# A mixture-of-experts loop with a fifth weight slot, and second-layer weights requested by ScalarE

## What is computed

```python
scores = sigmoid(x @ router_w)                       # 64 experts
eidx = top_8(group_limited(scores + router_bias))    # 8 experts per token
wts = sel / sum(sel) * 2.5
hb = silu(einsum('nd,edf->nef', xb, ex_w1)) * einsum('nd,edf->nef', xb, ex_w3)
routed = einsum('nef,efd->nd', hb * gates[..., None], ex_w2)
shared = einsum('nf,fd->nd', silu(x @ sh_w1) * (x @ sh_w3), sh_w2)
```

## Time and profile before

| | before |
|---|---|
| median of 3 runs | 1056.3 us |
| the profiled execution | 1055.14 us, its span 1053.4 us |
| mean granted TensorE clock | 0.986 |
| PE busy | 997.3 us, 95% of the span |
| DVE / ACT / POOL busy | 448.9 / 156.4 / 356.7 us |
| expert loop, from first to last matmul | 365.5 to 957.8 us |
| weights of the experts, from SyncE | 192 requests of 1024 KB |
| gathers and scatters, GpSimd's queue | 200 and 48 instructions, 37.8 MB |
| SyncE's queue | 258.1 MB |

### The profile page before, as it was taken

How to read it: one execution, slowest core, us unless ns; L and a number is a source line. 1 busy time by engine, 2 the same in 40 slices (tenths; PEclk the granted TensorE clock), 3 DMA queues, 4 the chain that set the end, 5 groups by cost and what they waited for, 6 DMA issues and landing times.

```text
span 1053.4 us, 16032 instructions
## 1 busy us (share of the span) xinstructions
PE 997.3 (95%) x5686; PEld 454.6 (43%) x5686; DVE 448.9 (43%) x1287; ACT 156.4 (15%) x383; POOL 356.7 (34%) x434
## 2 busy tenths in 40 slices
PE   5999999989999999999999989999889999999996
PEld 4777655655554433333333333333333333333443
DVE  4201222345549844344344343434433434442885
ACT  3110023301021101000010110001001010002322
POOL 5000320211024443433444443444444445441232
PEclk9999999999999999999999999999989999999999
DMA  9032223122159399999999999999999999987942
GB/s 296 18 92 80 81 85 83 63 61 67 40 152 378 117 359 402 410 403 410 394 411 410 412 404 389 406 391 407 412 401 372 393 412 405 381 342 258 422 160 80
DMA packets 76307, 296.43 MB, mean 281 GB/s; under 512 B 16251, under 2 KB 26683, under 8 KB 49382
## 3 DMA queue, kind: packets, MB, share of 16 engines
q1 hardware_dynamic: 59693, 258.14, 63.2%
q0 software_dynamic: 16576, 37.80, 9.4%
HBM read 277.08 MB, written 32.54 MB: 294 GB/s over the span
## 4 chain that ended last, share of the span: by engine, by line
PE 74%; DMA 12%; DVE 5%; issue 4%; POOL 2%; another core or an unknown queue 1%; ACT 1%; SPq 1%; DVEq 1%; POOLq 0%; ACTq 0%
PE bank L1881 22%; PE bank L2247 19%; PE bank L2228 8%; DMA mixpj<-in_ex_w 6%; PE bank L2250 6%; PE bank L2231 5%; PE bank L2311 5%; DMA arena<-xs_dram,slot 3%; PE bank L1887 2%; DMA arena<-y_dram 1%; PE bank L2260 1%; POOL arena L902 1%; PE bank L1967 1%; PE bank L1977 1%
## 5 line engine op out<-in xcount | busy, mean ns | idle before, releaser
L2247 PE MATMUL bank<-arena 128*32 128x512 f32 x1536 | 235.8, 609 | 17.9 <-issue 11.8
L902 POOL DMA_INDIRECT arena<-xs_dram,slot x200 | 216.8, 1084 | 70.7 <-issue 63.2
L2247 PE MATMUL bank<-mixpj,arena 128*32 128x512 f32 x512 | 234.5, 610 | 1.0 <-issue 0.9
L917 POOL DMA_INDIRECT y_dram<-arena,outrow x48 | 49.3, 1027 | 274.2 <-DVE slot L1683 231.9
L2247 PEld LDWEIGHTS bank<-arena 128*32 128x32 f32 x1536 | 63.9, 112 | 161.1 <-issue 158.0
L2228 PE MATMUL bank<-arena 128*32 128x512 f32 x640 | 118.1, 595 | 0.8 <-ACT arena L1124 0.8
L2250 PE MATMUL bank<-ring,arena 128*128 128x512 f32 x256 | 112.6, 593 | 0.9 <-DVE arena L1697 0.9
L1697 DVE STREAM_TRANSPOSE arena<-arena 128x1024 f32<-128x1024 f32 x50 | 62.2, 1244 | 73.9 <-DMA arena<-xs_dram,slot 69.7
L1881 PE MATMUL bank<-xT,ring 128*128 128x288 f32 x384 | 93.4, 406 | 0.0
L1881 PEld LDWEIGHTS bank<-xT,ring 128*128 128x128 f32 x384 | 72.9, 190 | 20.5 <-issue 0.5
L1750 DVE SCALAR_TENSOR_TENSOR arena<-bank,gate,arena 128x256 f32<-128x256 f32 x48 | 23.2, 484 | 130.2 <-ACT arena L1120 120.1
(11 more groups left out here) (397 smaller groups left out, 1173.1 us busy)
## 6 DMA issues: line engine op xcount, KB each, us to landing
arena<-in_ex_w SPq DMA_DIRECT2D x96, 1024.0 KB
ring<-in_ex_w SPq DMA_DIRECT2D x64, 1024.0 KB
mixpj<-in_ex_w SPq DMA_DIRECT2D x32, 1024.0 KB
arena<-y_dram SPq DMA_DIRECT2D x18, 1024.0 KB, 11.0
ring<-in_w_in SPq DMA_DIRECT2D x5, 2048.0 KB, 9.1
ring<-in_w_out SPq DMA_DIRECT2D x2, 2048.0 KB, 9.2
ring<-in_w_ple_gate SPq DMA_DIRECT2D x2, 2048.0 KB, 10.0
arena<-xs_dram,slot POOLq DMA_INDIRECT x200
```

Source lines behind the costliest of these rows:

```text
L902: pool.indirect_dma_start(xg[b][:, 256 * a:256 * a + 256], None, xs_quarter, bass.IndirectOffsetOnAxis(slot[k][:, a:a + 1], 0), bounds_che ...
L917: pool.indirect_dma_start(y_dram, bass.IndirectOffsetOnAxis(outrow[b][:, 0:1], 0), og[b], None, bounds_check=K * T - 1, oob_is_err=False). ...
L2247: ins = pe.matmul(bank[2][t, :], xgT[b][:, c, t], w13[k if lane < 3 else 3][:, :, wc, :], start=(c == 0), stop=(c == KT - 1))
```

## The change

The kernel gets a fifth slot. `w13` becomes ring, two homes, xT (slot 3, 4096 of its 4608 columns), mixpj (slot 4); the fifth piece of `w2s` is a new tile `wide` that holds `junk` and `g_b`. The steps with j % 3 == 0 alternate between slots 0 and 4; the others keep 1 and 2, and the shared expert slot 3. Order 3 is asked for when the shared expert's first layers have read xT and the order is known, before the projection's weights; order 4 is asked for at the place where order 3 was. The request for the alternating slot now fetches the expert of a period later. `w_pj` moves into the arena, `pT` into `g_a` and a new tile `pTs`, and ScalarE waits for the order before it copies the first part of pT, since `g_a` is read until then. `final_norm_g` is asked for near the end of the loop. SyncE's `period` keeps first-layer weights only; second-layer weights are asked for by ScalarE on its own queue, behind each step's copy into hT (`reload`). ScalarE's loop and the last periods are written out anew around that.

```diff
-        g_b = sb("g_b", [P, DM])
+        wide = sb("wide", [P, 2 * DM])
+        junk, g_b = wide[:, 0:DM], wide[:, DM:2 * DM]
...
-        w13 = [ring[:, 0, :]] + [t[:, 0:WORDS] for t in homes] + [mixpj[:, 0:WORDS]]
+        w13 = [ring[:, 0, :]] + [t[:, 0:WORDS] for t in homes] + [xT_flat[:, 0:WORDS], mixpj[:, 0:WORDS]]
...
-        w2s = [ring[:, 1, 0:2 * DM], ring[:, 1, 2 * DM:4 * DM]] + [t[:, WORDS:] for t in homes]
+        w2s = [ring[:, 1, 0:2 * DM], ring[:, 1, 2 * DM:4 * DM]] + [t[:, WORDS:] for t in homes] + [wide[:, :]]
...
-            return j % 3
+            return j % 3 or j // 3 % 2 * 4
...
-            sp.dma_start(g_b[:, :], bc(final_norm_g)).then_inc(s_gb, 16)
...
             after(sp, "sh", NT - 1)
-            for n in range(2):
-                sp.dma_start(w_pj[:, :, n], w_ple_proj[0, :, 512 * n:512 * n + 512].rearrange("(c p) n -> p c n", p=P)
-                             ).then_inc(s_pj, 16)
-            sp.wait_ge(s_np, 1)
-            passes = sp.value_load(np_i[0:1, 0:1], min_val=1, max_val=PASSES)
-            after(sp, "y", NT - 1, 0)
-            wait_drained(sp, "pT", NT - 1)
             sp.wait_ge(s_order, 2)
             e = expert(3)
             load13(3, e)
             load2(3, e)
-
-            def period(done, first, last):
-
-                e = expert(first(0))
-                sp.wait_ge(s_mm1, done + 1)
-                load13(0, e)
-                if last is not None:
-                    f = expert(last)
-                    sp.wait_ge(s_mm2, done)
-                    load2(2, f)
-                f, e = e, expert(first(1))
+            for n in range(2):
+                sp.dma_start(w_pj[:, :, n], w_ple_proj[0, :, 512 * n:512 * n + 512].rearrange("(c p) n -> p c n", p=P)
+                             ).then_inc(s_pj, 16)
+            e = expert(4)
+            after(sp, "y", NT - 1, 0)
+            wait_drained(sp, "pT", NT - 1)
+            load13(4, e)
+            load2(4, e)
...
+            def period(done, slot_f, place, more_f=True):
+
+                if more_f:
+                    e = expert(place(4))
+                    sp.wait_ge(s_mm1, done + 1)
+                    load13(slot_f, e)
+                e = expert(place(1))
                 sp.wait_ge(s_mm1, done + 2)
                 load13(1, e)
-                sp.wait_ge(s_mm2, done + 1)
-                load2(0, f)
-                f, e = e, expert(first(3))
+                e = expert(place(3))
                 sp.wait_ge(s_mm1, done + 3)
                 load13(3, e)
-                sp.wait_ge(s_mm2, done + 2)
-                load2(1, f)
-                f, e = e, expert(first(2))
+                e = expert(place(2))
                 sp.wait_ge(s_mm1, done + 3)
                 load13(2, e)
-                sp.wait_ge(s_mm2, done + 3)
-                load2(3, f)
...
-            e = expert(NE - 2)
-            sp.wait_ge(s_mm2, more * STEPS + (STEPS - 3))
-            load2(2, e)
-            sp.wait_ge(s_mm1, more * STEPS + (STEPS - 2))
+            period(more * STEPS + (STEPS - 9), 4, lambda k: NE - 8 + k)
+            period(more * STEPS + (STEPS - 6), 0, lambda k: NE - 4 + k, False)
+            sp.wait_ge(s_mm1, more * STEPS + (STEPS - 5))
             load_chunk("gt1")
+            sp.wait_ge(s_mm2, more * STEPS + (STEPS - 2))
+            sp.dma_start(g_b[:, :], bc(final_norm_g)).then_inc(s_gb, 16)
...
                 b = full_bank(act, "pT", i)
+                if i == 0:
+                    act.wait_ge(s_order, 2)
...
+            def load2(k, place):
+                e = act.value_load(order[0:1, bass.ds(place, 1)], min_val=0, max_val=NE - 1)
+                act.dma_start(w2s[k], rows2(e)).then_inc(s_w2[k], 16)
...
+            def reload(j, place, last=False):
+
+                if j % 3 == 0:
+                    load2(3, place(4 * (j // 3) + 3))
+                    load2(2, place(4 * (j // 3) + 2))
+                if j % 3 == 1 and not last:
+                    load2(j // 3 * 4, place(4 * (j // 3 + 2)))
+                if j % 3 == 2 and not (last and j > 3):
+                    load2(1, place(4 * (j // 3) + 5))
...
+            with act.Fori(1, passes * TURNS - 1) as n:
+                at = n * LOADS
                 for j in range(UNROLL):
...
+                    step(n * UNROLL, n * (UNROLL * 8), j)
+                    reload(j, lambda m: act.snap((at + m) % NE))
...
-                    pe.wait_ge(s_w2[k], used + ((j - 1) // 3 * 16 + 16))
                     if shares(j - 1):
+                        pe.wait_ge(s_w2[k], used + ((j - 1) // 3 * 16 + 16))
                         pe.wait_ge(s_w2[3], used + ((j - 1) // 3 * 16 + 16))
+                    else:
+                        pe.wait_ge(s_w2[k], used_f + 16)
```

More of the change, by code:

```diff
@@ L388, in decoder_step @@
         s_carried = sem("s_carried")
-        s_w13 = [sem(f"s_w13_{k}") for k in range(4)]
-        s_w2 = [sem(f"s_w2_{k}") for k in range(4)]
+        s_w13 = [sem(f"s_w13_{k}") for k in range(5)]
+        s_w2 = [sem(f"s_w2_{k}") for k in range(5)]
         s_order, s_weigh, s_split = sem("s_order"), sem("s_weigh"), sem("s_split")
@@ L648, in period @@
                 load13(2, e)
-                sp.wait_ge(s_mm2, done + 3)
-                load2(3, f)
-            period(0, lambda k: 4 + k, None)
-            with sp.Fori(0, passes * TURNS - 1) as turn:
+            period(0, 0, lambda k: 4 + k)
+            with sp.Fori(0, passes * TURNS - 2) as turn:
                 for h in range(2):
                     at = turn * LOADS + (LOADS + 4 * h)
-                    period(turn * UNROLL + (3 + 3 * h), lambda k: sp.snap((at + k) % NE), sp.snap((at + (NE - 2)) % NE))
+                    period(turn * UNROLL + (3 + 3 * h), 4 - 4 * h, lambda k: sp.snap((at + k) % NE))
@@ L1109, in _ @@
             passes = act.value_load(np_i[0:1, 0:1], min_val=1, max_val=PASSES)
[L1110 to L1124, removed]
-                for j in range(UNROLL):
[L1127 to L1130, removed]
-                out(r * STEPS + STEPS, r * (STEPS * 8) + STEPS * 8, 0)
@@ new lines, in out, with step @@
+            def out(base, half, j):
+                b = (j + 1) % 2
+                act.wait_ge(s_mm2, base + j)
+                act.wait_ge(s_scatter[b], half + (j + 1) // 2 * 16)
+                act.copy(og[b][:, 0:512], bank[5][:, :]).then_inc(s_out0, 1)
+            def load2(k, place):
+                e = act.value_load(order[0:1, bass.ds(place, 1)], min_val=0, max_val=NE - 1)
+                act.dma_start(w2s[k], rows2(e)).then_inc(s_w2[k], 16)
+            def step(base, half, j, first=False):
+                act.wait_ge(s_mm1, base + (j + 1))
+                act.activation(hs, bank[2][:, 0:FF], ACT.Silu).then_inc(s_silu, 1)
+                if not first:
+                    out(base, half, j)
+                act.wait_ge(s_pht, base + (j + 1))
+                act.copy(hT, bank[4][:, 0:2 * P].rearrange("p (c t) -> p c t", t=P)).then_inc(s_hT, 1)
@@ new lines, in reload @@
+            def reload(j, place, last=False):
[6 more added lines that the diff above has]
+                    load2(1, place(4 * (j // 3) + 5))
+            for j in range(UNROLL):
+                step(0, 0, j, j == 0)
+                if j:
+                    reload(j, lambda m: m)
@@ new lines, in _ @@
+            with act.Fori(1, passes * TURNS - 1) as n:
+                at = n * LOADS
+                for j in range(UNROLL):
+                    step(n * UNROLL, n * (UNROLL * 8), j)
+                    reload(j, lambda m: act.snap((at + m) % NE))
+            more = act.value_load(np_i[0:1, 1:2], min_val=0, max_val=PASSES - 1)
+            for j in range(UNROLL):
+                step(more * STEPS + (STEPS - UNROLL), more * (STEPS * 8) + (STEPS - UNROLL) * 8, j)
+                reload(j, lambda m: NE - LOADS + m, True)
@@ L1134, in square3 @@
+            out(more * STEPS + STEPS, more * (STEPS * 8) + STEPS * 8, 0)
             def square3(a):
@@ L2233, in mm2, with step @@
                     ins.then_inc(s_mm2, 1)
-                def step(base, used, j, first=False):
+                def step(base, used, used_f, j, first=False):
                     b = j % 2
                     k = own(j)
-                    pe.wait_ge(s_w13[k], used * 2 + (j // 3 * 32 + 32))
                     if shares(j):
+                        pe.wait_ge(s_w13[k], used * 2 + (j // 3 * 32 + 32))
                         pe.wait_ge(s_w13[3], used * 2 + (j // 3 * 32 + 32))
+                    else:
+                        pe.wait_ge(s_w13[k], used_f * 2 + 32)
                     pe.wait_ge(s_xgT, base + (j + 1))
@@ L2284, in pj_half @@
                 leave_loop(AT["pj", i, n] % 8)
-                reduce_over(b[:, :], lambda c: pT[:, c, tok(i)], lambda c: w_pj[:, c, n], 2).then_inc(filled, 1)
+                reduce_over(b[:, :], lambda c: pT(i)[:, c], lambda c: w_pj[:, c, n], 2).then_inc(filled, 1)
             def leave_loop(k):
```

32 lines of the change are left out of this document (19 added, 13 removed).

## The result

The changed kernel takes 1076.1 us (median of four, 1071.6 to 1081.8), the kernel before 1056.3 beside it: ratio 1.0191, 95% interval 1.0171 to 1.0211. The forecast of 1055 was wrong, and so was its range, which ended at 1067; the time lies above the 1062 to 1069 of the second rival too.

A forecast was written before the change was run, and what follows sets the result against it. It took DMA transfers at about 403 GB/s, 37.4 us a period, to bound the loop; +0.3 (start), 0, 0, +1.0 (ScalarE's queue) and -2.4 (end) summed to -1.1 us, forecast 1055.0, range 1045 to 1067.

The forecast's parts named there:

- the second rival: Loop: third queue delays the gather behind second steps' one-hots by 2.6 us; 38.4 a period, 1062 to 1069; chance 0.24.
- What bounds the kernel before: Expert loop: DMA transfers at their limit, about 403 GB/s, set the period; TensorE's own path is 1.6 us shorter.
- the two numbers of the argument: Loop period: 37.4 us set by transfers, 35.8 us for TensorE's own path behind the gathers.
- The fifth slot, and the end: Fifth slot: +0.3 us at the start, 0 in the loop; last period, one expert less to fetch: -2.4 us.
- ScalarE's term: Second-layer weights on ScalarE's queue: a load overtakes slot 3's once, not per period; +1.0 us, bounds 0 to 2.6.
- The count of experts ahead of slot 3's load: Loop: 4n experts stand ahead of that load before and after, so it lands at the same time; 0 us.
- SyncE without its waits for second layers: Loop: earlier requests can only fill the dip, 0.5 us a period, at most 7 us; taken as 0.
- ScalarE's requests as instructions: ScalarE, after hT's copy: two take 1.5 to 2.5 us in idle time; cost 0, uncovered up to 32 us.
- Rival 3: ScalarE: requests block in a full queue and delay Silu, or the change has no effect; 1055 to 1065; chance 0.06.
- its signs: Profile of after: transposes wait over 100 us, hole before second steps' picks, 38 or more, no slot 3 wait, share under 1.00.
- queues empty, and gathers are faster: Loop: argument against slower gathers: a TensorE held up sends fewer requests; DMA work stays the same.

The follow-up runs named there:

- e8: Kernel before, with one of a period's four second-layer requests (slot 1's) left out: 1032.5 us, ratio 0.977.
- e1: Kernel after, five slots kept, but SyncE asks for the second-layer weights again, in the order and behind the waits of before: 1052.5 us, ratio 0.9983.
- e6: Kernel after, with 12 filler matmuls of 128x128 ahead of the wait at the pick in every second step: 1073.4 us, ratio 1.017.
- e10: Kernel after, with ScalarE's request for slot 3, one of two behind the critical gather, left out: 1081.3 us, ratio 1.020.
- e9: Kernel after, with ScalarE's request for slot 1, the one ahead of the critical gather, left out: 1031.4 us, ratio 0.974.
- e5: Kernel after, with ScalarE's request for slot 1 made one step later, beside two others: 1091.1 us, ratio 1.034.

## Why the prediction was wrong

*What bounds the kernel before: right.* Leaving out 1.05 MB a period saves 24 us; freeing the pick saves nothing. Of the two numbers of the argument, e8 bears out that the 37.4 are the transfers'; its 35.7 fits the 35.8 of TensorE behind the gathers, but doesn't show it.

*The fifth slot, and the end: right.* The sum without ScalarE's term was -2.1 us. e1, which is just that (SyncE's waits, which it has, were priced at 0), measured 1052.5 against 1054.6; that the size is met so closely is luck, as the interval reaches from -3.2 to -0.4. The count of experts ahead of slot 3's load gave the loop's part as 0, and in e1 the second steps from the second to the fifteenth are 485.85 us apart (407.68 to 893.53), before 485.80; TensorE waits for slot 3 there, 19.5 us in five waits. The gain is at the end, as forecast: the last distance is 34.8 for 36.5, and 33.4 in the kernel after.

*SyncE without its waits for second layers:* no gain showed, and no run tries it alone. In the kernel after, the queue that was to be filled earlier runs dry instead.

*ScalarE's requests as instructions: right.* Two took 1.51 us, in an idle stretch; the Silu came as soon as the first layer was through. Rival 3 is out.

*The step that failed* is in the part on ScalarE's queue: "2.6 us later, once and not per period, as the rate is fixed. I take 1.0". I looked only at the weights that could be overtaken. The gathers are small and urgent and stand on a queue of their own; with a third queue outstanding the critical one took 10.3 us instead of 7.9 (medians), 2.4 more, close to the 2.6 of rival 2. That comes in every period, since it hangs on TensorE's path and not on the rate. The rate isn't a constant that the path can't touch: with TensorE held up, SyncE's requests, which wait for its first layers, go out later, and the share falls to 0.93. The term was not 1.0 us in all but some 22: the 19.8 by which the medians differ and the 2.1 that the rest gains (e1). In the profiled execution the loop loses 1.9 us a period beyond the 37.3, 26.5 in all.

*Rival 2 was right in place and mechanism*, down to its signs: over 100 us of waiting transposes, a hole before the picks of the second steps, 38 or more a period, no wait for slot 3. Its price of 38.4 a period was short of the 39.6 of the periods that wait: it left out that TensorE's clock falls behind the wait, with second layers 2.3 us longer a period (how much of that could be had back, e6 leaves open). The wait itself it put too high: 1.7 us of it stood in the 35.8 already (the pick of the step that begins at 407.55 comes 8.7 us after its start instead of 7.0), and with the 2.6 that would be 4.3; it came to 3.7. The reason for which I gave it 0.24, "queues empty, and gathers are faster", is refuted by e10: a share of 0.86 to 0.92, and the gather still takes 10.3 us, while in e9 it takes 7.1 at 0.92 to 0.99. It is slow because of what stands beside it at that moment, not because the engines are full on average.

The Trainium skill (DMA: Bandwidth & Descriptors, Queues, rings and completion order) lets each DMA engine take turns between the queues with work. The runs agree in direction: with SyncE's requests at like distances, the critical gather's median is 7.1 us where ScalarE had asked for nothing in the step before (e9) and 10.3 where it had (e10). No trace here shows a single engine's turns, so that this is the mechanism stays an inference.

## What to carry to other kernels

When a kernel is bound by transfers, look for a small transfer on the compute path before putting bulk loads on one more queue: what counts is which bulk request is outstanding beside it, and the spare time behind it (here 1.6 us a period). A transfer rate read as a bound holds only while no path on the engines is longer; price every added queue against the next path as well. And an in-order engine should wait for a transfer last, after the work that others wait for: one moved call gave back some 20 us.

## What was not expected of the hardware

Of equal bytes and nearly equal moments, one 1.05 MB request decides 50 us: 1031 without the one ahead of the gather, 1081 without the one behind it. Some gathers become quicker than the 7.9 us of the kernel before: 6.4 us in e5 and 6.3 for the third step's in the kernel after. In both SyncE's last requests are 15 to 18 us old when the gather's last one goes out, so this speaks for a queue that has run down and not for a gain from the third one. e9 has 7.1 where e8, with the same bytes and all weights on SyncE's queue, has 6.9 (14).
